# A decoder layer's first microseconds: the norm's weights as one row spread by TensorE, x ahead of the weights, first weight tiles in row halves

## Chip, cores and metric

The kernel runs on one core of one Trainium2 chip. The metric is the device time of one execution in microseconds (us); the time given for a kernel is the median of its runs. The profile is of one further execution.

## What is computed

One layer of a hybrid decoder on x of shape (1, 256, 1024) in float32. Only the first block matters here:

```python
def rms_norm(x, w):
    y = x * lax.rsqrt(jnp.mean(x * x, axis=-1, keepdims=True) + EPS)
    return y * w

def swiglu(h, w1, w3, w2):
    return (jax.nn.silu(h @ w1) * (h @ w3)) @ w2

h = rms_norm(x, ffn1_norm)
x = x + 0.5 * swiglu(h, ffn1_w1, ffn1_w3, ffn1_w2)
...
```

w1 and w3 are 1024 x 2816, w2 is 2816 x 1024. Behind this come a mixer (attention and a state-space part, with the input projection w_in and the output projection w_out), a second feed-forward block of the same form, and a last norm. They are not touched.

## The kernel before

**Tiles.** The 256 tokens are two tiles t of 128. D = 1024 is eight rows of tiles k (KD). F = 2816 is 22 tiles of 128, taken as 11 pairs i, each with an odd and an even tile (`odd`). Each operand of a product is held as a high and a low part (`w_hi`, `w_lo`, `hT_hi`, `hT_lo`, type fp32r), and `three` (L1100) issues three matmuls for each product of tiles: high x high, high x low and low x high (L1102 to L1104).

**Weights.** A weight load of a pair brings 1 MB to one of three slots of `raw`, one for each `kind`: 0 is w1, 1 is w3, 2 is w2. A slot has two halves, one for each `odd`. For each half ScalarE copies `raw` to `w_hi` (L453, `ffn_hi`), and VectorE subtracts to get `w_lo` (L771, `ffn_lo`) and increments `half_ready`. Pair 0 of the first block is loaded in halves (L308 to L317, in the order of `PAIR_ORDER`): w1 and w3 of `odd` 0, both pieces of x's second tile, w1 and w3 of `odd` 1, then the two halves of w2 and the constants (L318). For pair 1 SP waits before each kind until both halves of the slot were split (L325 to L327), and issues the load (`ffn_load`, L267).

**The norm.** ScalarE squares x with a sum (L477), POOL makes the inverse root `rstd` (L364, L367), VectorE multiplies x, rstd and the norm's weights (`scale_first`, L793) into `normed`. The norm's weights were loaded as a broadcast to 128 partitions (L306, 512 KB in SBUF). PE transposes `normed` (L1227, four transposes for each half of 512 columns, two banks); ScalarE copies the bank to `hT_hi` (L489), VectorE subtracts to get `hT_lo` (L814) and increments `hT_ready`.

**PE's order at the head** (`ffn`, L1175): five dummy matmuls of the identity (`keep_clock`, L1169), the transposes of tile 0, eleven dummies, then four products of pair 0, each of 24 matmuls of 256 columns that hold gate and up of one t and one `odd` side by side (`pair_product`, L1149): (t0, odd 0), the transposes of tile 1, (t0, odd 1), (t1, odd 0), (t1, odd 1). Then the gate of pair 1 (`gate_or_up`, L1137), the transposes of the pair's products (L1166), the up of pair 1, and from there pairs alternate: gate, up, and the down product with w2 of the half before.

**ScalarE's order at the head** (L548 to L564): squares of tile 0, w1 of `odd` 0, hT of tile 0, w3, squares of tile 1, the `odd` 1 halves of w1 and w3, hT of tile 1, then w2 (`first_hi(2)`, which waits for `first_loaded[2]`, and `ffn_hi(0, 0, 1, 2)`), and then `first_pair` (L522): the SiLU of (t0), a wait for `pair_used`, the copy of pair 1's w1, the SiLU of (t1), the copy of w3, and so on. VectorE's order mirrors it (L871 to L887, `first_pair` L848). All engines work their lists strictly in order, and all waits are semaphores written out by hand. Every load of the head is issued on SP's queue.

The lines that stand for the order of ScalarE:

```python
            first_hi(2)
            ffn_hi(0, 0, 1, 2)
            ffn_steps(0)
```

Of the kernel before, what the change touches and what calls it, by code (L numbers as in the profile page):

```python
# [37 lines left out]
PAIR_ORDER = ((0, 0), (0, 1), (1, 0), (1, 1), (0, 2), (1, 2))  # L38
# [43 lines left out]
def build(nc, x_in, w1s, w3s, w2s, norms, w_in, conv_w, conv_b, dt_bias, A_log, D_skip,  # L82
# [4 lines left out]
    with ExitStack() as ctx:  # L87
# [29 lines left out]

        gu = sb("gu", [P, SEQ])
# [44 lines left out]
        first_loaded = [sem(f"first_loaded{k}") for k in range(3)]  # L163
        consts_loaded = sem("consts_loaded")
# [96 lines left out]

        def mix_half(m):
            r = raw[:, (MIX_UNIT0 + m // 2) % RAW_SLOTS, :]
            src = cols_half(r, m % 2) if by_columns(m) else r[:, (m % 2) * HALF:(m % 2 + 1) * HALF]
            return MIX_HALF0 + m, (MIX_HALF0 + m) % HALF_SLOTS, src
# [31 lines left out]
        def _(sp):  # L297
# [8 lines left out]
            sp.dma_start(norm_w[:, 0, :], norms[0].partition_broadcast(P)).then_inc(norm_loaded[0], 16)  # L306

            for odd, kind in PAIR_ORDER:  # L308
                if (odd, kind) == (1, 0):
                    load_x(1, 0)  # L310
                    load_x(1, 1)
                if kind < 2:
                    src = (w1s, w3s)[kind][0].rearrange("(k p) f -> p k f", p=P)[:, :, odd * P:(odd + 1) * P]
                else:
                    src = w2s[0][odd * P:(odd + 1) * P, :]
                sp.dma_start(ffn_half(0, 0, odd, kind)[2], src).then_inc(
                    raw_loaded[kind] if odd else first_loaded[kind], 16)  # L317
            sp.dma_start(cst[:, P:], consts[:, P:]).then_inc(consts_loaded, 16)  # L318
            for n in range(2):
                for kind in range(3 * n):  # L320
                    if n == 1:
                        u = MIX_UNITS - 3 + kind
                        sp.wait_ge(half_ready, MIX_HALF0 + 2 * u + 2)
                    ffn_load(sp, n, 0, kind)
                for kind in range(3):  # L325
                    sp.wait_ge(half_ready, ffn_half(n, 0, 1, kind)[0] + 1)
                    ffn_load(sp, n, 1, kind)  # L327
                with sp.Fori(2, FI) as i:
                    for kind in range(3):

                        sp.wait_ge(half_ready, i * 6 + (FFN_HALF0[n] - 6 + 3 + kind + 1))
                        ffn_load(sp, n, i, kind)
                if n == 0:
                    for u in range(MIX_UNITS):

                        sp.wait_ge(half_ready, MIX_HALF0 - 3 + u + 1 if u < 3 else MIX_HALF0 + 2 * (u - 3) + 2)
                        mix_load(sp, u)
# [9 lines left out]
        def _(pool):  # L347
# [6 lines left out]

            step(pool.memset(minus_half[:, :], -0.5))
# [44 lines left out]
            for t in range(TT):  # L400
                rsqrt(2 * t + 2, t, D)

# [45 lines left out]
        def _(act):  # L448
# [11 lines left out]
            def first_hi(kind):  # L460
                _, slot, src = ffn_half(0, 0, 0, kind)
                split_hi(slot, src, first_loaded[kind], 16, kind < 2)

# [83 lines left out]

            for c in range(2):  # L548
                act.wait_ge(x_loaded[c], 16)
                square_x(0, 0, c)  # L550
            first_hi(0)
            norm_hi(0, 0)
            first_hi(1)
            for c in range(2):
                act.wait_ge(x_loaded[2 + c], 16)
                square_x(0, 1, c)
            ffn_hi(0, 0, 1, 0)
            ffn_hi(0, 0, 1, 1)
            norm_hi(0, 1)
# [196 lines left out]
        def _(dve):  # L756
# [29 lines left out]
            def scale_first(t):  # L786

                if t == 0:
                    dve.wait_ge(norm_loaded[0], 16)
                dve.wait_ge(rstd_ready, t + 1)  # L790
                for c, done in enumerate((scaled_left, scaled_right)):
                    cols = slice(c * 512, (c + 1) * 512)
                    dve.scalar_tensor_tensor(normed[:, t, cols], x[:, t, cols], rstd[:, t:t + 1], norm_w[:, 0, cols],  # L793
                                             ALU.mult, ALU.mult).then_inc(done, 1)

# [78 lines left out]
            ffn_lo(0, 0, 0, 0)  # L874
            norm_lo(0, 0)
            for c in range(2):
                dve.wait_ge(x_loaded[2 + c], 16)
            ffn_lo(0, 0, 0, 1)
            scale_first(1)
            ffn_lo(0, 0, 1, 0)  # L880
            ffn_lo(0, 0, 1, 1)
            norm_lo(0, 1)
# [216 lines left out]
        def _(pe):  # L1099
# [49 lines left out]
            def pair_product(n, t, odd):  # L1149
# [3 lines left out]
                for k in range(KD):  # L1153
                    if odd == 0 and k % 4 == 0:
                        pe.wait_ge(hT_ready, hT_count(2 * n) + 2 * t + k // 4 + 1)
                    last = three(dst, hT(k, tok(t)), tuple(w[:, s:s + 2, k * P:(k + 1) * P] for w in (w_hi, w_lo)),
                                 k == 0, k == KD - 1)
# [17 lines left out]
            def ffn(n):  # L1175

                if n == 0:
                    norm_transposes(0, 0)
                    keep_clock(11)
                h0 = FFN_HALF0[n]  # L1180
                pe.wait_ge(half_ready, h0 + 2)
                pair_product(n, 0, 0)
                norm_transposes(2 * n, 1)
                pe.wait_ge(half_ready, h0 + 4)
                pair_product(n, 0, 1).then_inc(pair_done, 1)
                pair_product(n, 1, 0).then_inc(pair_used, 1)
# [50 lines left out]

            pe.wait_ge(ident_loaded, 16)
            keep_clock(5)
# [358 lines left out]
```

## Time and profile before

| | us |
|---|---|
| median of three runs | 575.83 (575.68 to 576.07) |
| the profiled execution | 576.18 |
| its span in the trace | 574.4 |
| PE busy | 557.5 |
| DVE busy | 324.6 |
| ScalarE busy | 288.9 |
| POOL busy | 49.3 |

The span runs from the first to the last instruction; the execution's own time has some 1.8 us around it. Times in the rows are us from the span's start. PE is the matmul part of TensorE, PEld its weight loads, which lie beside matmuls. A matmul's start-to-start distance tells its cost in a row of many; its own duration is longer, since matmuls overlap. An SPq row is the issue of a transfer, and the landing comes some us later. DVE is VectorE, ACT is ScalarE, POOL is GpSimd.

### The profile page before, as it was taken

The numbers are of one execution on the slowest core, as the hardware profiler recorded it, in microseconds if no ns is written. First come the engines' busy times: TensorE is split into PE (matmuls) and PEld (weight loads), VectorE is DVE, ScalarE is ACT, GpSimd is POOL, SyncE is SP. The second block draws the span as 40 slices with busy tenths as digits, with TensorE's granted clock in tenths as the row PEclk, the third lists the DMA queues.
The fourth block names the chain that finished last, engine by engine and source line by source line (L and its number), as shares of the span: only waits on it lengthen the run. The fifth ranks groups of instructions, "written<-read, shape, count | busy, mean of one in ns | idle before, by whom it ended". The sixth has DMA issues, their size and how long they took to land.

```text
span 574.4 us, 9569 instructions
## 1 busy us (share of the span) xinstructions
PE 557.5 (97%) x3744; PEld 511.8 (89%) x3744; DVE 324.6 (57%) x434; ACT 288.9 (50%) x463; POOL 49.3 (9%) x86
## 2 busy tenths in 40 slices
PE   5999999999999999999999999999999999999994
PEld 5999999999999979998888788789999999999993
DVE  3655554544554584877676546575545554554544
ACT  4554453444444475867666755364443444453433
POOL 1000040000000020513340102010000000000001
PEclk9999999999999999999999999999999999999998
DMA  8935497655446737556323225353466655456601
GB/s 252 314 115 201 149 298 256 219 151 190 153 164 219 239 113 212 174 181 196 115 87 118 73 75 185 108 153 124 170 215 219 192 173 171 151 189 219 219 1 74
DMA packets 69448, 98.01 MB, mean 171 GB/s; under 512 B 1828, under 2 KB 55392, under 8 KB 69424
## 3 DMA queue, kind: packets, MB, share of 16 engines
q1 hardware_dynamic: 68576, 95.21, 50.5%
q0 software_dynamic: 848, 2.47, 1.4%
q8 instruction: 16, 0.26, 0.2%
q14 instruction: 8, 0.07, 0.0%
HBM read 96.62 MB, written 1.05 MB: 170 GB/s over the span
## 4 chain that ended last, share of the span: by engine, by line
PE 91%; DVE 3%; ACT 2%; DMA 1%; POOL 1%; issue 1%; SPq 0%; POOLq 0%; DVEq 0%; ACTq 0%
PE bank L1102 28%; PE bank L1103 28%; PE bank L1104 28%; DMA raw<-in_ffn_w 1%; PE bank L1227 1%; DVE w_lo L771 1%; ACT z_silu L477 1%; PE bank L1404 1%; POOL mean_sq L364 1%; DVE x L783 1%; PE bank L1403 1%; PE bank L1375 1%; PE bank L1376 1%; PE bank L1362 1%; PE bank L1374 0%
## 5 line engine op out<-in xcount | busy, mean ns | idle before, releaser
L771 DVE TENSOR_TENSOR w_lo<-raw,w_hi 128x1024 fp32r<-128x1024 f32 x176 | 211.1, 1229 | 146.1 <-ACT w_hi L453 145.4
L453 ACT ACTIVATE w_hi<-raw 128x1024 fp32r<-128x1024 f32 x176 | 179.6, 1054 | 110.5 <-PE bank L1104 71.0
L1102 PE MATMUL bank<-hT_hi,w_hi 128*128 128x256 f32 x736 | 208.5, 283 | 0.0
L1104 PE MATMUL bank<-hT_hi,w_lo 128*128 128x256 f32 x736 | 208.3, 283 | 0.0
L1103 PE MATMUL bank<-hT_lo,w_hi 128*128 128x256 f32 x736 | 208.2, 283 | 0.0
L1102 PEld LDWEIGHTS bank<-hT_hi,w_hi 128*128 128x128 f32 x736 | 141.1, 192 | 1.5
L1103 PEld LDWEIGHTS bank<-hT_lo,w_hi 128*128 128x128 f32 x736 | 141.1, 192 | 1.5
L1104 PEld LDWEIGHTS bank<-hT_hi,w_lo 128*128 128x128 f32 x736 | 141.1, 192 | 0.0
L1102 PE MATMUL bank<-w_hi,hT_hi 128*128 128x512 f32 (+1 forms) x192 | 69.5, 362 | 0.6 <-DVE w_lo L771 0.5
L1102 PE MATMUL bank<-w_hi,gu_hi 128*128 128x512 f32 x176 | 69.1, 393 | 0.3
L1103 PE MATMUL bank<-w_lo,gu_hi 128*128 128x512 f32 x176 | 69.0, 392 | 0.0
L1104 PE MATMUL bank<-w_hi,gu_lo 128*128 128x512 f32 x176 | 68.5, 389 | 0.0
L1104 PE MATMUL bank<-w_hi,hT_lo 128*128 128x512 f32 (+1 forms) x192 | 68.2, 355 | 0.0
L1103 PE MATMUL bank<-w_lo,hT_hi 128*128 128x512 f32 (+1 forms) x192 | 68.0, 354 | 0.0
L504 ACT ACTIVATE gu_hi<-gu 128x256 fp32r<-128x256 f32 x40 | 16.7, 418 | 90.7 <-DVE gu L828 85.0
L1102 PEld LDWEIGHTS bank<-w_hi,hT_hi 128*128 128x128 f32 x192 | 36.3, 189 | 5.7 <-DVE w_lo L771 1.3
L1104 PEld LDWEIGHTS bank<-w_hi,hT_lo 128*128 128x128 f32 x192 | 36.3, 189 | 5.3
L1103 PEld LDWEIGHTS bank<-w_lo,hT_hi 128*128 128x128 f32 x192 | 36.4, 189 | 4.3
L1104 PEld LDWEIGHTS bank<-w_hi,gu_lo 128*128 128x128 f32 x176 | 33.1, 188 | 7.2
L1102 PEld LDWEIGHTS bank<-w_hi,gu_hi 128*128 128x128 f32 x176 | 33.2, 189 | 6.8 <-issue 1.1
L1103 PEld LDWEIGHTS bank<-w_lo,gu_hi 128*128 128x128 f32 x176 | 33.2, 189 | 5.3
L364 POOL TENSOR_SCALAR mean_sq<-sumsq 128x1 f32<-128x1 f32 x8 | 4.8, 596 | 346.6 <-ACT z_silu L477 346.6
(164 smaller groups left out, 423.7 us busy)
## 6 DMA issues: line engine op xcount, KB each, us to landing
raw<-in_ffn_w SPq DMA_DIRECT2D x63, 1024.0 KB, 5.3
raw<-in_w_in SPq DMA_DIRECT2D x16, 1024.0 KB, 5.6
raw<-in_w_out SPq DMA_DIRECT2D x6, 1024.0 KB, 4.8
raw<-in_ffn_w SPq DMA_DIRECT2D x6, 512.0 KB, 7.6
x<-in_x SPq DMA_DIRECT2D x4, 256.0 KB, 4.1
out_x<-normed SPq DMA_DIRECT2D x4, 256.0 KB, 2.1
norm_w<-in_ffn_norm SPq DMA_DIRECT2D x1, 512.0 KB, 6.0
norm_w<-in_mix_norm POOLq DMA_DIRECT2D x1, 512.0 KB, 5.3
```

Of the source, the lines that this page charges most:

```text
L364: step(pool.tensor_scalar(m, sumsq[:, 0, col:col + 1], sumsq[:, 1, col:col + 1], EPS, ALU.add, ALU.add))
L453: act.activation(by_tile(dst) if columns else dst, src, ACT.Copy).then_inc(hi_ready, 1)
L477: act.activation(z_silu[:, t, cols], x[:, t, cols], ACT.Square, scale=D ** -0.5, accum_out=sumsq[:, c, r:r + 1]).then_inc(sq_ready, 1)
L504: act.activation(gu_hi[:, odd, :], gu[:, :], ACT.Copy).then_inc(gu_hi_ready, 1)
L771: dve.tensor_tensor(lo, src, hi, ALU.subtract).then_inc(half_ready, 1)
L783: dve.scalar_tensor_tensor(xs, bank[:, 2 * t + c, :], 1.0 if n == 2 else 0.5, xs, ALU.mult, ALU.add).then_inc(x_ready, 1)
L1102: pe.matmul(dst, lhs[0], rhs[0], start=start, stop=False, skip_group_check=True)
L1103: pe.matmul(dst, lhs[0], rhs[1], start=False, stop=False, skip_group_check=True)
L1104: return pe.matmul(dst, lhs[1], rhs[0], start=False, stop=stop, skip_group_check=True)
L1227: last = pe.transpose(bank[:, bank_n, k * P:(k + 1) * P], normed[:, t, col + k * P:col + (k + 1) * P], ident)
L1362: pe.matmul(b[:, 0:384], select_r[:, h:h + 1].to_broadcast([P, P]), csT[:, :], start=True, stop=False, skip_group_check=True)
L1375: pe.matmul(bank[:, 7, o], m[:, P:SEQ], x_tok[:, 0, c], start=True, stop=False)
```

## The change

- The first norm's weights are loaded as one row of 4 KB (`norm_row`) from ScalarE's queue. POOL sets 128 ones (`ones_row`, in a place of `mix_w` that is used much later); PE multiplies the column of ones with the row, two fp32 matmuls of 512 columns into banks 2 and 3 (`spread_norm`). `scale_first` reads these banks. The five dummies ahead of the transposes go.
- SP issues both tiles of x before any weights. w1 and w3 of pair 0, `odd` 0, come as four pieces (rows k = 0 to 3 of both, then 4 to 7), and are copied and split by piece. One of the four subtractions goes from VectorE to POOL.
- ScalarE does the squares of both tiles first, then hT of tile 0 and the pieces in turn, then hT of tile 1 and the `odd` 1 halves.
- PE issues 5 dummies in place of 11 between transposes and product; starts the first product when the upper pieces are there (`first_top_ready`); issues tile 1's transposes in the middle of the first product; and does (t1, odd 0) before (t0, odd 1).
- The two halves of w2 of pair 0 and the constants are issued on SP in front of the wait for pair 1's w2, which is behind the waits and loads of pair 1's w1 and w3. The order in which ScalarE and VectorE handle w2 is as before.

```diff
--- before.py
+++ after.py
@@ -35,7 +35,6 @@
 RAW_SLOTS, HALF_SLOTS = 3, 6
 HALF = 1024
 FT = F // P
-PAIR_ORDER = ((0, 0), (0, 1), (1, 0), (1, 1), (0, 2), (1, 2))
 FI = FT // 2
 
 
@@ -115,6 +114,9 @@
         rstd = sb("rstd", [P, 10])
         minus_half = sb("minus_half", [P, 1])
 
+        norm_row = norm_w[0:1, 0, :]
+        ones_row = mix_w[0:1, D:D + P]
+
         gu = sb("gu", [P, SEQ])
         gu_hi = sb("gu_hi", [P, 2, SEQ], f32r)
         gu_lo = sb("gu_lo", [P, 2, SEQ], f32r)
@@ -161,6 +163,12 @@
         x_loaded = [sem(f"x_loaded{j}") for j in range(2 * TT)]
         ident_loaded = sem("ident_loaded")
         first_loaded = [sem(f"first_loaded{k}") for k in range(3)]
+        first_top_loaded = [sem(f"first_top_loaded{k}") for k in range(2)]
+        first_top_hi = sem("first_top_hi")
+        first_top_ready = sem("first_top_ready")
+        first_low_ready = sem("first_low_ready")
+        ones_ready = sem("ones_ready")
+        norm_spread = sem("norm_spread")
         consts_loaded = sem("consts_loaded")
         params_loaded = sem("params_loaded")
         mix_w_loaded = sem("mix_w_loaded")
@@ -259,6 +267,13 @@
             number = 6 * i + (FFN_HALF0[n] + (slot if first else 3 * odd + kind))
             return number, (FFN_HALF0[n] + slot) % HALF_SLOTS, src
 
+        def first_part(t, low):
+
+            return by_tile(t)[:, 4 * low:4 * low + 4, :]
+
+        def first_src(kind, low):
+            return ffn_half(0, 0, 0, kind)[2][:, 4 * low:4 * low + 4, :]
+
         def mix_half(m):
             r = raw[:, (MIX_UNIT0 + m // 2) % RAW_SLOTS, :]
             src = cols_half(r, m % 2) if by_columns(m) else r[:, (m % 2) * HALF:(m % 2 + 1) * HALF]
@@ -303,19 +318,15 @@
             load_x(0, 0)
             load_x(0, 1)
             sp.dma_start(cst[:, C_ID:C_ID + P], consts[:, C_ID:C_ID + P]).then_inc(ident_loaded, 16)
-            sp.dma_start(norm_w[:, 0, :], norms[0].partition_broadcast(P)).then_inc(norm_loaded[0], 16)
-
-            for odd, kind in PAIR_ORDER:
-                if (odd, kind) == (1, 0):
-                    load_x(1, 0)
-                    load_x(1, 1)
-                if kind < 2:
-                    src = (w1s, w3s)[kind][0].rearrange("(k p) f -> p k f", p=P)[:, :, odd * P:(odd + 1) * P]
-                else:
-                    src = w2s[0][odd * P:(odd + 1) * P, :]
-                sp.dma_start(ffn_half(0, 0, odd, kind)[2], src).then_inc(
-                    raw_loaded[kind] if odd else first_loaded[kind], 16)
-            sp.dma_start(cst[:, P:], consts[:, P:]).then_inc(consts_loaded, 16)
+            load_x(1, 0)
+            load_x(1, 1)
+            for low in range(2):
+                for kind in range(2):
+                    src = (w1s, w3s)[kind][0].rearrange("(k p) f -> p k f", p=P)[:, 4 * low:4 * low + 4, 0:P]
+                    sp.dma_start(first_src(kind, low), src).then_inc((first_loaded if low else first_top_loaded)[kind], 16)
+            for kind in range(2):
+                src = (w1s, w3s)[kind][0].rearrange("(k p) f -> p k f", p=P)[:, :, P:2 * P]
+                sp.dma_start(ffn_half(0, 0, 1, kind)[2], src).then_inc(raw_loaded[kind], 16)
             for n in range(2):
                 for kind in range(3 * n):
                     if n == 1:
@@ -323,6 +334,11 @@
                         sp.wait_ge(half_ready, MIX_HALF0 + 2 * u + 2)
                     ffn_load(sp, n, 0, kind)
                 for kind in range(3):
+                    if n == 0 and kind == 2:
+                        for odd in range(2):
+                            sp.dma_start(ffn_half(0, 0, odd, 2)[2], w2s[0][odd * P:(odd + 1) * P, :]).then_inc(
+                                raw_loaded[2] if odd else first_loaded[2], 16)
+                        sp.dma_start(cst[:, P:], consts[:, P:]).then_inc(consts_loaded, 16)
                     sp.wait_ge(half_ready, ffn_half(n, 0, 1, kind)[0] + 1)
                     ffn_load(sp, n, 1, kind)
                 with sp.Fori(2, FI) as i:
@@ -352,6 +368,7 @@
                 ins.then_inc(pool_step, 1)
                 pool.wait_ge(pool_step, steps[0])
 
+            pool.memset(ones_row, 1.0).then_inc(ones_ready, 1)
             step(pool.memset(minus_half[:, :], -0.5))
             step(pool.memset(cs_rows[:, :, :], 0.0))
             step(pool.memset(bias_col[:, :], 0.0))
@@ -399,6 +416,12 @@
 
             for t in range(TT):
                 rsqrt(2 * t + 2, t, D)
+
+
+            _, slot, _ = ffn_half(0, 0, 0, 0)
+            pool.wait_ge(hi_ready, 1)
+            pool.tensor_tensor(first_part(w_lo[:, slot, :], 1), first_src(0, 1),
+                               first_part(w_hi[:, slot, :].bitcast(f32), 1), ALU.subtract).then_inc(first_low_ready, 1)
 
             pool.wait_ge(down_done, 6)
             pool.dma_start(wdt[:, :, :], w_in[:, D_IN - SH:D_IN].rearrange("(k p) f -> p k f", p=P)).then_inc(params_loaded, 16)
@@ -461,6 +484,11 @@
                 _, slot, src = ffn_half(0, 0, 0, kind)
                 split_hi(slot, src, first_loaded[kind], 16, kind < 2)
 
+            def first_rows_hi(kind, low):
+                act.wait_ge((first_loaded if low else first_top_loaded)[kind], 16)
+                act.activation(first_part(w_hi[:, ffn_half(0, 0, 0, kind)[1], :], low), first_src(kind, low),
+                               ACT.Copy).then_inc(hi_ready if low else first_top_hi, 1)
+
             def mix_hi(m):
                 if HALF_SLOTS <= m < MIX_HALVES:
                     act.wait_ge(half_used, m - HALF_SLOTS + 1)
@@ -545,18 +573,22 @@
                 ffn_step(n, FI - 1, 0)
 
 
+            act.dma_start(norm_row, norms[0].rearrange("(a d) -> a d", a=1)).then_inc(norm_loaded[0], 16)
             for c in range(2):
                 act.wait_ge(x_loaded[c], 16)
                 square_x(0, 0, c)
-            first_hi(0)
-            norm_hi(0, 0)
-            first_hi(1)
             for c in range(2):
                 act.wait_ge(x_loaded[2 + c], 16)
                 square_x(0, 1, c)
+            hT_hi_part(hT_count(0) + 1, T_BANKS[0], 0, 0)
+            first_rows_hi(0, 0)
+            hT_hi_part(hT_count(0) + 2, T_BANKS[1], 4, 0)
+            first_rows_hi(1, 0)
+            first_rows_hi(0, 1)
+            first_rows_hi(1, 1)
+            norm_hi(0, 1)
             ffn_hi(0, 0, 1, 0)
             ffn_hi(0, 0, 1, 1)
-            norm_hi(0, 1)
             first_hi(2)
             ffn_hi(0, 0, 1, 2)
 
@@ -785,13 +817,19 @@
 
             def scale_first(t):
 
-                if t == 0:
-                    dve.wait_ge(norm_loaded[0], 16)
                 dve.wait_ge(rstd_ready, t + 1)
                 for c, done in enumerate((scaled_left, scaled_right)):
+                    if t == 0:
+                        dve.wait_ge(norm_spread, c + 1)
                     cols = slice(c * 512, (c + 1) * 512)
-                    dve.scalar_tensor_tensor(normed[:, t, cols], x[:, t, cols], rstd[:, t:t + 1], norm_w[:, 0, cols],
+                    dve.scalar_tensor_tensor(normed[:, t, cols], x[:, t, cols], rstd[:, t:t + 1], bank[:, 2 + c, :],
                                              ALU.mult, ALU.mult).then_inc(done, 1)
+
+            def first_rows_lo(kind, low):
+                slot = ffn_half(0, 0, 0, kind)[1]
+                dve.wait_ge(*((hi_ready, kind + 1) if low else (first_top_hi, kind + 1)))
+                return dve.tensor_tensor(first_part(w_lo[:, slot, :], low), first_src(kind, low),
+                                         first_part(w_hi[:, slot, :].bitcast(f32), low), ALU.subtract)
 
             def weigh_x(n, t, c):
 
@@ -871,15 +909,18 @@
             for c in range(2):
                 dve.wait_ge(x_loaded[c], 16)
             scale_first(0)
-            ffn_lo(0, 0, 0, 0)
-            norm_lo(0, 0)
+            hT_lo_part(hT_count(0) + 1, T_BANKS[0], 0, 0)
+            first_rows_lo(0, 0).then_inc(first_top_ready, 1)
+            hT_lo_part(hT_count(0) + 2, T_BANKS[1], 4, 0)
+            first_rows_lo(1, 0).then_inc(first_top_ready, 1)
             for c in range(2):
                 dve.wait_ge(x_loaded[2 + c], 16)
-            ffn_lo(0, 0, 0, 1)
             scale_first(1)
+            dve.wait_ge(first_low_ready, 1)
+            first_rows_lo(1, 1).then_inc(half_ready, 2)
+            norm_lo(0, 1)
             ffn_lo(0, 0, 1, 0)
             ffn_lo(0, 0, 1, 1)
-            norm_lo(0, 1)
             ffn_lo(0, 0, 0, 2)
             ffn_lo(0, 0, 1, 2)
 
@@ -1153,6 +1194,9 @@
                 for k in range(KD):
                     if odd == 0 and k % 4 == 0:
                         pe.wait_ge(hT_ready, hT_count(2 * n) + 2 * t + k // 4 + 1)
+                    if n + t + odd == 0 and k == 4:
+                        norm_transposes(0, 1)
+                        pe.wait_ge(half_ready, 2)
                     last = three(dst, hT(k, tok(t)), tuple(w[:, s:s + 2, k * P:(k + 1) * P] for w in (w_hi, w_lo)),
                                  k == 0, k == KD - 1)
                 return last
@@ -1174,16 +1218,22 @@
 
             def ffn(n):
 
+                h0 = FFN_HALF0[n]
                 if n == 0:
                     norm_transposes(0, 0)
-                    keep_clock(11)
-                h0 = FFN_HALF0[n]
-                pe.wait_ge(half_ready, h0 + 2)
+                    keep_clock(5)
+                    pe.wait_ge(first_top_ready, 2)
+                else:
+                    pe.wait_ge(half_ready, h0 + 2)
                 pair_product(n, 0, 0)
-                norm_transposes(2 * n, 1)
+                if n == 1:
+                    norm_transposes(2 * n, 1)
+                if n == 0:
+                    pair_product(n, 1, 0).then_inc(pair_used, 1)
                 pe.wait_ge(half_ready, h0 + 4)
                 pair_product(n, 0, 1).then_inc(pair_done, 1)
-                pair_product(n, 1, 0).then_inc(pair_used, 1)
+                if n == 1:
+                    pair_product(n, 1, 0).then_inc(pair_used, 1)
                 pair_product(n, 1, 1).then_inc(pair_done, 1)
                 gate_or_up(n, 1, 0, 0)
                 for t in range(TT):
@@ -1235,8 +1285,16 @@
                         pe.wait_ge(hT_ready, hT_count(n) + j + 1)
                     transpose_rows(t, 512 * j, T_BANKS[j])
 
+            def spread_norm():
+
+                pe.wait_ge(ones_ready, 1)
+                pe.wait_ge(norm_loaded[0], 16)
+                for c in range(2):
+                    pe.matmul(bank[:, 2 + c, :], ones_row, norm_row[:, c * 512:(c + 1) * 512],
+                              start=True, stop=True).then_inc(norm_spread, 1)
+
+            spread_norm()
             pe.wait_ge(ident_loaded, 16)
-            keep_clock(5)
             ffn(0)
```

## Rows read from the trace of the kernel before

**Rows 1.** the page: busy time of each engine, TensorE's granted clock.

```profile
PE 557.5 (97%) x3744; PEld 511.8 (89%) x3744; DVE 324.6 (57%) x434; ACT 288.9 (50%) x463; POOL 49.3 (9%) x86
...
PEclk9999999999999999999999999999999999999998
```

**Rows 2.** waits, first 60 us, of PE: engine, line <- releaser: us, times, longest.

```profile
PE bank L1227 <- DVE normed L793: 2.2, 1, 2.2
...
PE bank L1102 <- DVE w_lo L771: 0.5, 1, 0.5
```

**Rows 3.** windows: span, length, busy us (instructions) of each engine, PEclk, DMA share, GB/s.

```profile
4.49:7.00 2.51, 2.50 (x10) 2.21 (x10) 0.00 (x0) 0.49 (x2) 0.87 (x2) 1.00 0.85 213
9.16:14.50 5.34, 5.34 (x25) 5.34 (x26) 3.74 (x5) 4.19 (x8) 0.00 (x0) 1.00 1.09 316
...
19.52:28.25 8.73, 8.73 (x72) 8.73 (x73) 5.15 (x6) 4.78 (x6) 0.00 (x0) 1.00 1.01 346
567.30:570.80 3.50, 0.00 (x0) 0.00 (x0) 2.63 (x5) 1.82 (x6) 1.39 (x2) 1.00 0.35 132
570.80:574.40 3.60, 0.00 (x0) 0.00 (x0) 0.14 (x1) 0.36 (x1) 0.00 (x0) 0.51 0.44 165
```

**Rows 4.** timeline of SP's queue: start, us, instruction (a DMA is issued there).

```profile
0.74 0.87 SPq L300 DMA_DIRECT2D x<-in_x  x2
1.66 0.42 SPq L305 DMA_DIRECT2D cst<-in_shape_constants  x1
2.12 0.43 SPq L306 DMA_DIRECT2D norm_w<-in_ffn_norm  x1
...
18.35 1.51 SPq L276 DMA_DIRECT2D raw<-in_ffn_w  x2
```

**Rows 5.** DMA issues in short windows, by time: KB, last the us to landing.

```profile
x<-in_x SPq DMA_DIRECT2D x1, 256.0 KB, 2.6
...
cst<-in_shape_constants SPq DMA_DIRECT2D x1, 64.0 KB, 2.8
...
norm_w<-in_ffn_norm SPq DMA_DIRECT2D x1, 512.0 KB, 6.0
...
raw<-in_ffn_w SPq DMA_DIRECT2D x1, 1024.0 KB, 5.3
...
raw<-in_ffn_w SPq DMA_DIRECT2D x1, 1024.0 KB, 8.5
```

**Rows 6.** timeline of ScalarE (ACT), in brackets the idle time before and its releaser.

```profile
11.23 1.07 ACT L489 ACTIVATE hT_hi<-bank 128x512 fp32r<-128x512 f32 x2
...
21.59 1.28 ACT L520 ACT_TABLE_LOAD   x1
22.89 0.39 ACT L520 ACTIVATE z_silu<-bank 128x256 f32<-128x256 f32 x1
25.58 1.06 ACT L453 ACTIVATE w_hi<-raw 128x1024 fp32r<-128x1024 f32 x1 [2.31 <-PE bank L1104]
```

**Rows 7.** timeline of VectorE (DVE).

```profile
8.35 1.41 DVE L793 SCALAR_TENSOR_TENSOR normed<-x,rstd,norm_w 128x512 f32<-128x512 f32 x2 [8.35 <-DMA norm_w<-in_ffn_norm]
...
12.51 1.28 DVE L814 TENSOR_TENSOR hT_lo<-bank,hT_hi 128x512 fp32r<-128x512 f32 x2
...
26.67 1.23 DVE L771 TENSOR_TENSOR w_lo<-raw,w_hi 128x1024 fp32r<-128x1024 f32 x1 [2.94 <-ACT w_hi L453]
```

**Rows 8.** timeline of all engines: the inverse root, first transposes, first product.

```profile
5.55 0.57 POOL L367 TENSOR_TENSOR rstd<-mean_sq,minus_half 128x1 f32<-128x1 f32 x1
...
9.16 1.97 PE L1227 MATMUL bank<-cst,normed 128*128 128x128 f32 x8 [2.17 <-DVE normed L793]
...
15.00 0.36 PE L1102 MATMUL bank<-w_hi,hT_hi 128*128 128x256 f32 x1
```

**Rows 9.** POOL's 128x512 multiplication, by source line: ns min/median/max.

```profile
L427 POOL TENSOR_TENSOR normed<-x_tok,small x4: 1044/1194/2025, 265.3 to 271.5; 128x512 f32<-128x512 f32 x4
```

**Rows 10.** DMA rate of the first 60 us in 40 slices.

```profile
GB/s 0 243 251 177 284 326 326 325 301 305 355 331 122 246 387 340 350 371 348 66 0 0 0 0 53 315 330 89 379 382 410 150 0 0 0 59 339 373 354 264
```

## Prediction

> **What bounds the kernel now.** I read the page first. TensorE (PE) is busy for 97% of the span and its granted clock is high in nearly every slice [rows 1], so only two things can move the end: work taken off PE, or time in which PE stands still or runs slowly. PE's waits come next. At the head it waits 2.2 us for the normalised row block, and later 0.5 us for a split weight half; between 19.5 and 60 us there is no other wait [rows 2]. The windows say the same of the part that matters: from 19.52 to 28.25 us PE is busy throughout with 72 matmuls, which is the last three of the four first products, at 0.12 us each [rows 3]. The change's products are complete at 28.25 us. I call that moment G: the first matmul of the next step (gate_or_up for pair 1) starts there. Everything behind G is the same work in the same order in both kernels, so **the change is worth what it does to G**, plus what it does to the clock.
>
> Why is G not earlier? The SP queue's issues and their landings [rows 4, 5] show it: x (first tile) is issued at 0.74 us; the broadcast norm weights, issued at 2.12 us, land 6.0 us later, at 8.1, though the first piece of x landed at 3.4. DVE waits for them until 8.35 us [rows 7], and PE's transposes start at 9.16. All weights stand in the queue behind them. The first product starts at 15.00 [rows 8].
>
> **Part 1, norm weights as a row.** Removed: a 512 KB transfer that held the queue from the landing just ahead of it (the identity, 1.66 + 2.8 = 4.46 us [rows 4, 5]) to 8.1 us, 3.7 us. Added: one 4 KB DMA from ScalarE's queue at about 0.73, ahead of the table load, which still ends (about 2.4) before x arrives at 3.37; one memset on POOL (0.1 us, hidden); two fp32 matmuls of 512 columns. No row has such a load; from below 2 us, from above the 2.6 us of x's first piece [rows 5]; I take 2.6, so 3.35. No row has such a matmul either: the dummies are 128 columns in two records of 0.213 us at the low clock (ten in 2.50 us [rows 3]), so 512 columns are 2 x 0.85 = 1.7 us, two are 3.4: spread at 5.0 and 6.9 us. It replaces five dummies. rstd is ready at 6.12 as before [rows 8], so DVE scales the left half from 6.2 and the right from 6.9 to 7.5 us (no row of this stretch has that operation with a PSUM operand; hT_lo reads a bank of the same size at 0.64 each, so PSUM costs nothing: 0.7 each as before [rows 7]). PE's transposes: 6.9 to 8.7 instead of 9.16 to 10.9.
>
> **Part 2, x ahead, row halves.** at 346 GB/s [rows 3] a 256 KB piece takes 0.76 us. x's second tile lands at about 5.2 and 5.9, then, with 0.1 of slack for each, the four halves at 6.8, 7.6, 8.4, 9.2 and the second columns at 10.9 and 12.5. ScalarE: squares until 6.7; a transposed block is in PSUM 1.1 us after its start (of the eight records, 1.97 us, the first four [rows 8]), at 8.0; then hT, w1 top, hT, w3 top, w1 low, w3 low at 0.54 each (two hT copies take 1.07 [rows 6]) end at 11.3. DVE behind it at 0.64 each (two in 1.28 [rows 7]) gives first_top_ready at 11.15. **PE's first product starts at 11.2 instead of 15.0.** Five dummies (2.1 us) fill 8.7 to 10.8. DVE then scales tile 1 (to 12.5) and waits for POOL's subtraction: 128x512 on POOL takes 1.2 us, up to 2.0 [rows 9], started at 10.8, done at 12.0 to 12.8, so it costs 0 to 0.3. half_ready 2 comes at 13.2; PE, after 12 matmuls (1.45) and eight transposes (1.0), wants it at 13.6. No stall.
> hT of tile 1: ScalarE 13.3 to 14.4, then the second columns' copies until 16.4; DVE finishes those halves at T3 = 16.7 and T4 = 17.9. PE finishes pair (t1, odd 0) at 18.1 and wants T4 then. So all four products end at **23.9 us, 4.35 ahead of G**. With PE warm that is all the head could give.
>
> **Part 3, w2 behind w1 and w3 of pair 1.** This is the diff's quiet move, and it decides. Before, both halves of w2 were issued without a wait, right behind w1's and w3's. Now they and the constants stand on SP behind two waits (half_ready 3 and 4), and behind two 1 MB loads. Until T3 SP issues nothing, so DMA idles from 12.5 to 16.7. ScalarE's order is unchanged: first_hi(2) and the copy of the other w2 half come **before** pair_silu and before the copy of pair 1's w1. What waits there: ScalarE whole, behind it DVE, behind it PE's gate at G. Landings: a 1 MB load with nothing ahead takes 5.3 us [rows 5], so w1(1) at 22.0. w3(1) follows 3.0 us later at 346 GB/s [rows 3], or 4.4 as before (18.35 + 5.3 = 23.65 against 19.5 + 8.5 = 28.0 [rows 4, 5]). Each w2 half adds 1.5 at that rate. The last w2 half thus lands between 28.0 and 29.5; I take **28.7**.
> From there ScalarE and DVE run in series: copy 1.06; table load to SiLU 1.30 and SiLU 0.35 (21.59, 22.89, the next copy behind it); w1(1) copied and split 2.32 (25.58 to 27.90) plus 0.05 [rows 6, 7]. That is 5.05 us: gate at **33.75 us, 5.5 later than G**. PE stands still from 23.9 to 33.75.
>
> **Part 4, the clock.** PE's clock in the records falls to 0.51 from 570.80 on, 3.5 us after the last matmul of 567.3 [rows 3]. (The same column shows 1.00 before the first record, where the spacing of 0.213 us per 256 cycles says 1.2 GHz.) A 9.9 us hole therefore brings the 1.2 GHz level. Of the way back, the rows show one: transposes and dummies without pause from 9.16, and 2.4 GHz at 14.5, after 5.34 us; 2.5 us of dummies at 4.49 had not been enough [rows 3, 8]. At the low level a 256-column matmul takes 0.213 instead of 0.12, 0.44 us lost per us. Bounds 2.5 x 0.44 = 1.1 and 10.0 (4.49 to 14.5) x 0.44 = 4.4; the nearest row is the rise after 5.34 us: **2.3 us**.
> Behind this nothing else is late: w2(1), w1(2) keep their places relative to the gate, and a slower PE gives them more room.
>
> **A page against the rows.** The rows give 12.0 us from T3 to the last landing of about 3.15 MB. The Trainium skill (DMA: Bandwidth & Descriptors, "Anatomy of one DMA") fits a DMA as about 2.0 us plus bytes at 436 GB/s; taken for the four loads as one stream, an estimate by that page is 9.2 us, landing 25.9, gate 5.05 later at 30.95, which is G + 2.7, and with 2.3 for the clock 580.8 in place of the forecast. Its fit is for another issuing path, and the busy stretch here shows 346 GB/s.
>
> **Sum.** +5.5 (G) + 2.3 (clock) = +7.8 us. Against the profiled execution, 576.18, that is 584.0; it stands 0.35 above the median of the three runs, 575.83. From the median: **583.6 us**.
>
> **Rivals.**
> *A, faster:* the w2 loads do not queue behind pair 1's. The point that decides is the last w2 half's landing: 23.2 us is break-even (28.25 minus 5.05). If each load ran by itself, the last, issued at 18.8, would land 3.2 after that (x's 256 KB took 2.6), at 22.0: gate at 27.05, G - 1.2, a hole too short to matter: 574.6. For it: PE's earlier start is real. Against: 3.15 MB from 16.7 to 23.2 would be 485 GB/s without any latency; one queue has taken its loads in order so far [rows 5]. 5%.
> *B, the hole costs only itself:* clock kept or back at once: +5.5, 581.3. Against: the fall 3.5 us after the last matmul. 10%.
> *C, a faster stream:* x's first piece took 2.6 us, 0.6 of it data at that rate, so a start costs 2.0; then 3.15 MB at 410 GB/s, the highest slice [rows 10], 7.7: landing 26.4, gate 31.45, +3.2 + 2.3 = 581.3. For it: DMA starts from empty. 12%.
> *D, a cold first product:* the dummies fall from 11 to 5. If the one-row spread matmuls do not lift the clock, 5.34 us of continuous work count only from 6.9, and the rise may come behind the first 12 products and the eight transposes: T3 later by 12 x 0.093 + 8 x 0.1 = 1.9 us at most, the rest follows: 585.5. 12%.
> *E, no effect* (the order of issue does not come out as written): 575.8. 1%.
> On D and part 4 the Trainium skill (TensorE: Matmul & The Clock Gate, Part 1) adds that the number of matmuls run cold differs between runs of one kernel; by it the three runs should scatter more than before. Only rows enter the numbers.
>
> **Chances.** Forecast 60%, A 5, B 10, C 12, D 12, E 1. Range: B and C's low side with a short cold stretch (w1(1) at 22.0, 2.1 MB more at 410 GB/s, 27.1, G + 3.9, + 1.1 = 580.8) down to 580.5; above, D with the slow landing (29.5): 585.5 + 0.8, and some of the longer cold stretch, 587.0. A change of 0.2% (1.15 us) is about what a measurement of this kernel can tell from none. Faster by over 0.2%: 0.04; within: 0.02; slower: 0.94.
>
> **What would show it.** Right: norm_w waits gone, first real product near 11.2, four products done near 24, then one PE wait of about 10 us whose releaser is w_lo behind w_hi behind a raw load; ScalarE idle up to about 27 to 28 us waiting for DMA; a DMA hole from 12.5 to 18.7; 1.2 GHz after the hole. Wrong: the w2 halves landing before 23 us, no PE wait there, or G near 24.

## The result and the profile after

| | kernel before | changed kernel |
|---|---|---|
| median of the comparison, us | 575.95 (4 runs, 575.68 to 576.38) | 585.95 (4 runs, 584.03 to 586.07) |
| profiled execution, us | 576.18 | 586.01 |
| its span, us | 574.4 | 583.9 |

The ratio is 1.0166 (95% interval 1.0147 to 1.0185): the change makes the kernel slower. The predicted 583.6 us was 2.35 too low, inside its range of 580.5 to 587.0.

The page of the changed kernel, its head and TensorE's granted clock, as in [rows 1]:

```profile
span 583.9 us, 9543 instructions
PE 560.2 (96%) x3726; PEld 511.9 (88%) x3726; DVE 324.2 (56%) x435; ACT 289.4 (50%) x465; POOL 50.7 (9%) x88
...
PE   7769999999999999999999999989999999999994
...
PEclk9969999999999999999999999999999999999998
```

A slice is 14.6 us. In the second and third, where the page of before had PE at 9 and 9, it now has 7 and 6, and the third has a low clock (6). The first digit is better than before, 7 against 5: the head does start earlier. The waits of PE between 20 and 60 us say where the rest is (columns as in [rows 2]):

```profile
PE bank L1143 <- DVE w_lo L803: 10.2, 1, 10.2
```

And the waits of all engines in the first 60 us say whose work PE lacked:

```profile
DVE w_lo L803 <- ACT w_hi L476: 17.8, 7, 11.1
ACT w_hi L476 <- DMA raw<-in_ffn_w: 16.2, 4, 11.5
```

One wait of 10.2 us, and behind it a chain: PE waits for VectorE's low part, VectorE for ScalarE's high part, ScalarE for a load. ScalarE's timeline shows which (as in [rows 6]):

```profile
15.29 2.00 ACT L476 ACTIVATE w_hi<-raw 128x1024 fp32r<-128x1024 f32 x2
28.77 1.06 ACT L476 ACTIVATE w_hi<-raw 128x1024 fp32r<-128x1024 f32 x1 [11.48 <-DMA raw<-in_ffn_w]
30.02 1.06 ACT L476 ACTIVATE w_hi<-raw 128x1024 fp32r<-128x1024 f32 x1 [0.19 <-DMA raw<-in_ffn_w]
31.09 1.28 ACT L548 ACT_TABLE_LOAD   x1
32.39 0.39 ACT L548 ACTIVATE z_silu<-bank 128x256 f32<-128x256 f32 x1
32.67 1.05 ACT L476 ACTIVATE w_hi<-raw 128x1024 fp32r<-128x1024 f32 x1
```

The copies at 28.77 and 30.02 are the two w2 halves; the one at 32.67 is pair 1's w1, written w1(1) below (w3(1) likewise), which PE's gate needs. The issues on SP's queue, as in [rows 4]:

```profile
5.20 3.91 SPq L329 DMA_DIRECT2D raw<-in_ffn_w  x2
17.64 1.50 SPq L291 DMA_DIRECT2D raw<-in_ffn_w  x2
19.19 1.47 SPq L339 DMA_DIRECT2D raw<-in_ffn_w  x2
```

The landings of the four loads behind the pause, in short windows, as in [rows 5]:

```profile
raw<-in_ffn_w SPq DMA_DIRECT2D x1, 1024.0 KB, 5.4
...
raw<-in_ffn_w SPq DMA_DIRECT2D x1, 1024.0 KB, 8.7
...
raw<-in_ffn_w SPq DMA_DIRECT2D x1, 512.0 KB, 9.6
...
raw<-in_ffn_w SPq DMA_DIRECT2D x1, 512.0 KB, 9.8
```

SP issues nothing between 9.1 and 17.64 us. Pair 1's w1 is issued then and lands 5.4 later, at 23.0. The last w2 half, issued at about 20.2, lands at 30.0. So pair 1's w1 lay in SBUF for 9.6 us before ScalarE touched it. The windows around the hole, as in [rows 3]:

```profile
24.86:35.02 10.16, 0.00 (x0) 0.00 (x0) 4.15 (x5) 5.94 (x7) 0.00 (x0) 0.59 0.51 181
35.02:40.41 5.39, 5.38 (x25) 5.38 (x26) 1.42 (x2) 0.00 (x0) 0.00 (x0) 0.50 0.30 122
40.41:46.00 5.59, 5.59 (x40) 5.18 (x39) 3.39 (x4) 2.76 (x4) 0.00 (x0) 1.00 0.00 0
```

PE does nothing for 10.2 us, then 25 matmuls at 1.2 GHz, and only from 40.41 on 2.4 GHz again. The head itself came out early. The first transposes and the first product of the changed kernel, against 9.16 and 15.00 in [rows 8]:

```profile
7.11 1.94 PE L1277 MATMUL bank<-cst,normed 128*128 128x128 f32 x8 [1.12 <-DVE normed L825]
...
11.41 0.58 PE L1143 MATMUL bank<-w_hi,hT_hi 128*128 128x256 f32 x1 [0.23 <-DVE w_lo L831]
```

### The profile page after: what moved, and what is told of

It is laid out like the page before. It is cut to its first block, busy times and chain, and to the rows that moved or that the text cites. A ratio compares the mean times of both kernels' runs of the same rounds, so it can differ in the third digit from the quotient of the medians.

```text
span 583.9 us, 9543 instructions
## 1 busy us (share of the span) xinstructions
PE 560.2 (96%) x3726; PEld 511.9 (88%) x3726; DVE 324.2 (56%) x435; ACT 289.4 (50%) x465; POOL 50.7 (9%) x88
## 4 chain that ended last, share of the span: by engine, by line
PE 90%; DVE 3%; DMA 2%; ACT 2%; POOL 1%; issue 1%; SPq 0%; POOLq 0%; DVEq 0%; ACTq 0%
PE bank L1143 27%; PE bank L1144 27%; PE bank L1145 27%; DMA raw<-in_ffn_w 2%; PE bank L1277 1%; DVE w_lo L803 1%; ACT z_silu L505 1%; PE bank L1462 1%; DVE x L815 1%; PE bank L1461 1%; POOL mean_sq L381 1%; PE bank L1433 1%; PE bank L1434 1%; PE bank L1420 1%; DMA x<-in_x 1%
## 5 line engine op out<-in xcount | busy, mean ns | idle before, releaser
L1143 PE MATMUL bank<-hT_hi,w_hi 128*128 128x256 f32 x736 | 209.7, 285 | 10.2 <-DVE w_lo L803 10.2
L532 ACT ACTIVATE gu_hi<-gu 128x256 fp32r<-128x256 f32 x40 | 16.7, 419 | 86.5 <-DVE gu L866 80.8
```

Of the source, the lines that this page charges most:

```text
L532: act.activation(gu_hi[:, odd, :], gu[:, :], ACT.Copy).then_inc(gu_hi_ready, 1)
L1143: pe.matmul(dst, lhs[0], rhs[0], start=start, stop=False, skip_group_check=True)
```

## The experiments

Each was timed beside the kernel before on the same chip. The median of the kernel before was 575.92 us beside the two kernels that move w2's loads, the dummies in the hole and the norm row alone; 575.88 beside the late loads in another order, the row with x ahead and the two versions at the end that beat both; 576.08 beside the spare semaphores. Line numbers in the rows are each kernel's own.

### w2 back in its place in the changed kernel

```diff
 sp.dma_start(ffn_half(0, 0, 1, kind)[2], src).then_inc(raw_loaded[kind], 16)
+for odd in range(2):
+    sp.dma_start(ffn_half(0, 0, odd, 2)[2], w2s[0][odd * P:(odd + 1) * P, :]).then_inc(
+        raw_loaded[2] if odd else first_loaded[2], 16)
+sp.dma_start(cst[:, P:], consts[:, P:]).then_inc(consts_loaded, 16)
...
-                    if n == 0 and kind == 2:
...
```

> The changed kernel with the two w2 halves and the constants issued right behind the odd-1 pieces of w1 and w3, ahead of SP's waits. My theory (w2's place in the queue is the whole loss): last w2 half lands near 17 us, w1(1) near 23, its copy and split end near 25.4, so the gate of pair 1 starts at 25.4; w3(1) lands near 27.5, split at 29.8 against a wish at 28.7, a second wait of about 1 us. Net 1.5 to 2 us better than the kernel before: about 574.2. Rival (the head's other parts cost something too, or the clock falls in the small holes): 575.8 or above. Rival D (w2 is not the cause): still near 584 to 586.

Measured: 575.01 us (11 runs), ratio 0.9986 (0.9977 to 0.9995). The place of w2 is worth 10.9 us. PE's waits between 20 and 60 us:

```profile
PE bank L1142 <- DVE w_lo L802: 1.7, 2, 0.9
```

The first product starts at 11.40 as in the changed kernel. The gate waits 0.9 us and starts at 25.42, and the up product waits 0.8 us until 29.76, since w1(1) landed at 22.96 and w3(1) at 27.36. So a head that starts 3.6 us earlier gives 0.9. Of the 0.8 us by which this falls short of what I expected, 0.35 lies outside the span (below).

### w2 late in the kernel before

```diff
-for odd, kind in PAIR_ORDER:
+for odd, kind in PAIR_ORDER[:4]:
...
 for kind in range(3):
+    if n == 0 and kind == 2:
...
     sp.wait_ge(half_ready, ffn_half(n, 0, 1, kind)[0] + 1)
```

> The kernel before with only the w2 halves and the constants moved behind the waits for pair 1's w1 and w3, as in the change. My theory: w1(1) lands near 23.6, w3(1) near 28, the last w2 half near 30.6, gate near 35.6 instead of 28.25, plus 2.3 for the clock: about 585.5, nearly all of the changed kernel's time. Rival (the loss comes from the earlier head colliding with the loads): within 2 us of 575.8.

Measured: 586.0 us (585.15 to 586.49), ratio 1.0176 (1.0162 to 1.0190). This one move makes the whole loss, with the head of the kernel before. The timeline of its PE at the gate:

```profile
27.77 0.28 PE L1108 MATMUL bank<-w_hi,hT_lo 128*128 128x256 f32 x1
35.47 0.58 PE L1106 MATMUL bank<-hT_hi,w_hi 128*128 128x256 f32 x1 [7.42 <-DVE w_lo L775]
```

Its window behind the hole, in which the clock is at 0.50:

```profile
35.60:41.00 5.40, 5.40 (x26) 5.40 (x27) 1.28 (x2) 0.00 (x0) 0.00 (x0) 0.50 0.26 106
```

The gate starts at 35.47, 0.4 us later than in the changed kernel, although the products start 3.2 us later (14.62 against 11.41): the hole swallows what the head gains.

### Late loads, but ScalarE does not stand at them

```diff
 # ScalarE, head
-first_hi(2)
-ffn_hi(0, 0, 1, 2)
...
 # ScalarE, first_pair, behind gu_hi of the pair
+if n == 0:
+    first_hi(2)
+    ffn_hi(0, 0, 1, 2)
```

VectorE has the same move, and the counts of `hi_ready` and `half_ready` in the waits are renumbered. With them SP's wait in front of pair 1's own w2 comes to stand for a later step.

> The changed kernel with the w2 loads left where the change put them, but ScalarE and VectorE handle the two w2 halves behind pair 1's first w1 and w3 and behind the pair's transposes, and the counts in the waits are renumbered to fit. If the loss is that ScalarE, strictly in order, stands at w2 with pair 1's w1 landed at 23: the gate starts near 25.4, w3's wait about 1 us, w2's landing near 30 is in time for the down product at 32.7: about 575. Rival (w2's late landing itself stops PE, whatever the order): a PE wait of several us at the down product, 579 or more.

Measured: 575.27 us (11 runs), ratio 0.9991 (0.9982 to 1.0000). PE's waits between 20 and 60 us:

```profile
PE bank L1143 <- DVE w_lo L803: 1.7, 2, 0.9
PE bank L1143 <- ACT conv_acc L528: 0.4, 1, 0.4
```

The w2 halves land at 28.91 and 30.15 us, as late as in the changed kernel, and 10.7 us of loss are gone. Late landing alone costs at most some 0.3 us here (575.27 against 575.01 with the loads back in their place). What costs is that engines with a strict list stand at a late load with work for PE behind it. ScalarE and VectorE were moved together, so this does not show which of the two lists would have been enough to stop PE.

### Dummies in the hole

```diff
+if n == 0:
+    keep_clock(44)
 gate_or_up(n, 1, 0, 0)
```

> The changed kernel with 44 dummy matmuls in PE's hole before pair 1's gate (44 x 0.223 = 9.8 us at the high clock, the hole is 10.2). The waits stay; the gate starts at 35.0 as in the changed kernel, but at 2.4 GHz: the cold stretch of 5.4 us and its 2.4 us go, 583.6 instead of 586.0. Rival (the clock costs nothing of its own, because the stretch behind the gate is bound by something else): 586.0. If the dummies themselves run at the low clock they end late, near 43, and it is slower, 590 or more.

Measured: 582.97 us (4 runs, 582.94 to 583.23), ratio 1.0128 (1.0113 to 1.0144): 3.0 us less than the changed kernel. The gate in PE's timeline:

```profile
34.34 0.39 PE L1143 MATMUL bank<-hT_hi,w_hi 128*128 128x256 f32 x1 [0.45 <-DVE w_lo L803]
34.56 0.28 PE L1144 MATMUL bank<-hT_lo,w_hi 128*128 128x256 f32 x1
34.68 0.28 PE L1145 MATMUL bank<-hT_hi,w_lo 128*128 128x256 f32 x1
```

Matmuls follow at 0.12 us from the second on. The profiled pair differs by 3.1 us, and 0.7 of it is not due to the dummies: the last w2 half landed at 29.30 instead of 30.00, because w1(1) was issued at 16.89 instead of 17.64. That goes back to the clock at the head, where the two kernels are the same (the row reached PE at 2.24 us there and at 2.60 here). The first twelve matmuls took 2.28 us in the changed kernel (11.41 to 13.69, the start of the transposes) and 1.54 here:

```profile
11.61 0.28 PE L1144 MATMUL bank<-w_lo,hT_hi 128*128 128x256 f32 x1
...
12.93 1.03 PE L1279 MATMUL bank<-cst,normed 128*128 128x128 f32 x8
```

The remaining 2.4 us are the clock behind the hole.

### The norm row alone

The kernel before with `norm_row`, `ones_row`, the spread and 5 dummies in place of 11 (the first five go); all loads in the order of before.

```diff
-sp.dma_start(norm_w[:, 0, :], norms[0].partition_broadcast(P)).then_inc(norm_loaded[0], 16)
...
+act.dma_start(norm_row, norms[0].rearrange("(a d) -> a d", a=1)).then_inc(norm_loaded[0], 16)
...
-keep_clock(11)
+keep_clock(5)
```

> The kernel before with the norm row and its spread alone (no first five dummies, 5 instead of 11 behind the transposes); x, w1, w3, w2 in the order of before. The broadcast's 3.7 us leave the queue, w3's half lands near 8.2, x's second tile near 9.2, the first product starts at about 11.3 to 12, the four products end about 24.7, w1(1) lands by 21 and w3(1) by 25: no new wait, about 572.3. Rival (the halves and x ahead are needed for the gain, or PE's first products run cold): 574 to 575.8.

Measured: 573.89 us (7 runs), ratio 0.9970 (0.9959 to 0.9981): faster than before by 2.0 us. That is 1.6 us short of what I expected, and 1.1 us better than the whole changed head with w2 in its place (575.01), of which 0.35 lies outside the span. PE's waits of the first 60 us:

```profile
PE bank L1246 <- DMA norm_w<-in_ffn_norm: 2.3, 1, 2.3
PE bank L1232 <- DVE normed L798: 1.6, 1, 1.6
PE bank L1107 <- DVE w_lo L776: 1.5, 2, 0.9
```

The first product starts at 12.53, after a wait of 0.9 us: w3's half lands at 8.86 (11.83 in the kernel before), but ScalarE puts hT ahead of it and copies it only at 10.07, and VectorE splits it from 11.25 on. Another 0.6 us go at 17.16, where the odd halves wait behind tile 1's normalisation.

### The row with x ahead, whole halves

```diff
+load_x(1, 0)
+load_x(1, 1)
 for odd, kind in PAIR_ORDER:
-    if (odd, kind) == (1, 0):
-        load_x(1, 0)
-        load_x(1, 1)
```

> e3_row_only with both tiles of x ahead of all weights, whole halves as before. w1's and w3's halves land about 1.4 us later (8.5 and 10.2), and the first product waits for w3: it starts 1 to 1.4 us later than in e3, about 575.0; so x ahead costs unless the pieces are halved. Rival (x earlier frees VectorE's order, rstd of tile 1 no longer stops it at 13.4): same as e3, 573.9, or better.

Measured: 576.55 us (11 runs, 575.38 to 577.5), ratio 1.0008 (0.9999 to 1.0017): 2.7 us worse than the row alone. Expected was 1.1. Its windows:

```profile
10.50:14.10 3.60, 0.10 (x1) 0.00 (x0) 3.55 (x4) 3.60 (x8) 0.41 (x1) 0.88 1.15 322
14.10:20.10 6.00, 6.00 (x28) 6.00 (x29) 3.67 (x4) 1.50 (x2) 0.69 (x2) 0.50 0.55 188
```

w3 landed at 11.19, the product began at 14.10 after PE had stood for 3.5 us, and ran at 1.2 GHz until 20.1: 28 matmuls and transposes at 0.21 us in place of 0.12. Five dummies end at 10.6, too early for a product that comes this late; this kernel was not run with eleven. With whole halves, then, x ahead costs. No run shows that it pays with the row pieces either: both together, with w2 in its place, gave 575.01 us, 1.1 more than the row alone. The missing dummies are a risk of their own (rival D's, in another kernel).

### A version that beats both: w1's odd half in the idle time

On top of w2 in its place:

```diff
 # ScalarE (VectorE the same with _lo)
 first_rows_hi(1, 1)
+ffn_hi(0, 0, 1, 0)
 norm_hi(0, 1)
-ffn_hi(0, 0, 1, 0)
 ffn_hi(0, 0, 1, 1)
```

> e1_w2_early with one more swap: ScalarE and VectorE handle w1's odd-1 half in their idle time before tile 1's hT instead of behind it. My theory (with w2 in its old place the head is bound by the raw slots: pair 1's w1 and w3 can only be loaded when pair 0's odd halves are split): half_ready 3 comes near 14.9 instead of 17.4, w1(1) lands near 20.4, w3(1) near 25, both PE waits of e1 (1.2 and 1.0 us) go, the gate starts near 24.8: 2 us better than e1, about 573. Rival (the queue serves the later loads no sooner, or the swap delays tile 1's hT by as much): 574.5 to 575.5.

Measured: 573.08 us (5 runs, 572.52 to 574.37), ratio 0.9949 (0.9935 to 0.9963). Pair 1's w1 was issued at 14.81 instead of 17.36, as the slots became free earlier. In the profiled run, the slowest of the five, it landed at 23.17 all the same and PE still waited 1.1 us at the gate, so this trace does not show where the median's gain comes from; the next one does.

With two dummies more, between the spread and the transposes:

```diff
 pe.wait_ge(ident_loaded, 16)
+keep_clock(2)
```

> e5_odd_first with two dummies (0.85 us at the low clock) in PE's gap between the spread and the transposes. If the clock rises earlier for having no gap, the first product's cold matmuls (about 5 to 8, 0.09 us each) go: 0.5 us better than e5. Rival (the spread's one-row matmuls or the moment of the rise do not care): same as e5 within 0.3 us.

Measured: 572.97 us (5 runs, 572.80 to 573.02), ratio 0.9949 (0.9936 to 0.9963). The medians cannot tell it from the last kernel. In its profile w1(1) landed at 21.01, and PE has no wait between the first product and 60 us; these are its waits of the first 60 us:

```profile
PE bank L1292 <- DMA norm_w<-in_ffn_norm: 2.2, 1, 2.2
PE bank L1142 <- DVE w_lo L830: 1.2, 1, 1.2
```

Its matmuls are at the short distance from 9.2 us on, ahead of the first product, against 12.1 in the last kernel. The product still began at 11.54, as VectorE sets it, so little is saved: the first twelve matmuls took 1.53 us in place of 1.68.

Of the 2.9 us by which this version beats the kernel before, the row alone gives 2.0. The swap of w1's odd half was not tried on the row alone.

### Spare semaphores

```diff
+spare = [sem(f"spare{j}") for j in range(7)]
```

> The kernel before with seven more semaphores that nothing uses. In the profiled executions the time outside the span was 1.78 us for the kernel before and for the row alone (1.8), 2.1 to 2.2 for all kernels with the change's seven further semaphores. If the count of semaphores sets it, this run's time minus its span is about 2.1, and the time 576.2. Rival (it is the length of the instruction lists or something else): 1.8, and 575.9.

Measured: 576.15 us (10 runs), ratio 1.0001 (0.9991 to 1.0011), span 574.1, outside the span 1.76 to 1.82 us in every run. The theory of semaphores falls. All kernels with the whole change have 2.09 to 2.21 us outside the span, all others 1.75 to 1.87; what in the change makes those 0.35 us stays open.

## Why the prediction was right, point by point

**What decides.** Right, and shown from both sides: w2's move alone gives 586.0, its return alone takes 10.9 us away. That the path leads through the order of ScalarE and VectorE, not through the w2 data, is shown by the kernel that keeps the late loads and loses only the order. (Where the prediction says that the change's products are complete at 28.25 us, the row is the kernel before's; G is used rightly.)

**G.** Forecast 33.75 us, measured 35.03; +6.8 in place of +5.5. The step that was mis-sized is the landing of the last w2 half, 28.7 against 30.0; the 5.05 us behind it measured 5.03 (the prediction's terms as written add up to 5.08). Two terms made the 1.3. Pair 1's w1 was issued at 17.64, not at T3 = 16.7: the transposes of tile 1 came behind 12 matmuls that took 2.28 us, not 1.45, as some eight ran cold, and hT of tile 1 started at 14.32 where I had 13.3. In the kernel with the hole filled the same head ran warm, and w1(1) was issued at 16.89, near the forecast. And w3(1) came 4.4 us behind w1(1), my slow bound (27.47 against 23.07), where I had summed with a middle, while each w2 half took 1.3 us, not 1.5. Together 0.95 for T3 and 0.35 for the landings behind it.

**The first product.** Forecast 11.2, measured 11.41. That it is so close is in part luck: the four pieces landed at 8.27, 9.17, 10.07 and 10.97, where I had 6.8, 7.6, 8.4 and 9.2, and x's second tile at 5.97 and 7.38, not 5.2 and 5.9. ScalarE had other work until the first three had landed, so nothing on the way to the product waited for them. All four products ended at 24.8, forecast 23.9. The gain in the head was real; it ended in the hole.

**The clock.** Forecast 2.3 us from a rise after 5.34 us; the cold stretch was 5.39 us with 25 records, 25 x 0.093 = 2.3. The step held, and filling the hole took it away. That the length agreed to 0.05 us is luck: it was taken from one row. Behind the hole of the kernel before with w2 late the low clock lasted 5.5 us (35.47 to 41.0), and 6.0 in the kernel with x ahead and whole halves.

**The sum.** 6.8 + 2.3 = 9.1 of the 9.5 us by which the span grew. From the gate to the first down product the changed kernel takes 8.64 us against 6.20, which is 2.4, not 2.3, and 0.2 is a wait for `mix_m` much later that the kernel before does not have. Another 0.33 lies outside the span (2.11 against 1.78), which no step of mine had.

**The rivals.** A (loads that do not queue) and C (a faster stream) fall by the landings. B falls: the clock fell in the hole. D is half true: the distance of the matmuls falls from 0.213 to 0.12 us only at 13.1, after the first product's start; eight were cold, 8 x 0.093 = 0.7 us. All twelve matmuls up to the transposes took 2.28 us. PE's list up to there is the same in the kernels with w2 back in its place, with the late loads in another order and with the hole filled, and there they took 2.00, 2.22 and 1.54 us. So the size is not fixed by the kernel, and what sets it stays open. D's price, 0.8 of its 1.9 us, is the larger part of the 1.3 us by which the forecast of G missed.

**The page against the rows.** By the fit of the Trainium skill (DMA: Bandwidth & Descriptors, "Anatomy of one DMA") the four loads would have been in after 9.2 us, an estimate from its figures. The trace shows 12.4 (17.64 to 30.0), so the fit, made for another issuing path, does not carry over to this queue. The Trainium skill's page TensorE: Matmul & The Clock Gate (Part 1) says that the number of matmuls run cold differs between runs of one kernel. The traces agree as far as they go, with the four equal heads above. That the runs scatter more because of the hole, as the prediction took from it, is not shown. The changed kernel's 2.0 us come from one run of four (584.03, at a mean granted clock of 0.987 against 0.985 to 0.988 in the others), and kernels without such a hole scatter by 1.6 us (the kernel before, 17 runs) and 1.7 us (the late loads in another order, 11 runs).

## What to carry to other kernels

Before moving a load behind a wait, look at every engine that handles its data and ask what stands behind that step in the engine's own list; here a load that PE needed only some 7 us behind its gate (33.0 against 25.7 in the reordered kernel) stopped the copy that PE needed at once. A start that is 3.6 us earlier is worth only as much as the next load in the chain comes earlier: the order in which buffers come free (here the odd half of w1) decided 2 of the 3 us, by the medians. A hole of 10 us in PE is paid twice, by itself and by 2.3 to 2.4 us of slow matmuls behind it. And a change of many parts is worth taking apart: the norm row alone (573.89) beats the whole head with w2 in its place.

## What the runs showed of the hardware that was not expected

In the kernel before, a broadcast of 4 KB to 128 partitions landed 3.7 us behind the load ahead of it, where a w1 half of the same size in SBUF took 2.1 and w3's 1.6 behind it; without it w3's half landed 3.0 us earlier (8.86 against 11.83). The same 4 KB as one row reached PE at 2.24 us, 1.5 after its issue, sooner than any of x. The fp32 spread cost 0.85 us for a record of 512 columns at 1.2 GHz, four in a row, as worked out from the 128-column dummies. In the kernel with x ahead and whole halves the clock fell in 3.5 us without a matmul (10.6 to 14.1). It had been up before: the ten dummy records just ahead took 1.77 us there and 2.34 in the changed kernel. In four kernels with the same list on PE, begun at 2.2 to 2.6 us, the rise at the head came at 11.4 (at the latest), 12.5, 13.0 and 13.1 us, by the distance of their matmuls. The landing time of the same 1 MB load behind the same queue varied between two nearly equal kernels from 6.0 (15.04 to 21.01) to 8.4 us (14.81 to 23.17), more than the whole gain of some edits.
